# Layer norm sums moved, delta gates on GpSimd, beta behind the inverse, fills in eighths, two row turns held

## The reference, cut to what matters

```python
h = rms_norm(x, norm_w)
(aq, ak, av, az, c_glu, cz, dq, dk, dvv, dz, db, da, gate_logits) = split(h @ w_in)
# conformer branch
u = a * sigmoid(g);  u = causal_depthwise_conv(u, dw_w) + dw_b
u = layer_norm(u, ln_w, ln_b);  u = silu(u) * silu(cz);  y_c = u @ w_conv_out
# gated delta branch
q, k, v = silu(short_conv(dq | dk | dvv));  q, k = l2_normalize(q), l2_normalize(k)
beta = sigmoid(db)
g = -exp(a_log) * softplus(da + dt_bias)
# inside the delta rule, per head and chunk of rows; g is summed along the chunk
lower = strict((k * beta) @ k.T * decay);  tri = lower + eye
u, w = triangular_solve(tri, [v * beta, k * beta * exp(g)])
# merge
x = x + (g_a * y_a + g_c * y_c + g_d * y_d) @ w_out
```

## Time and profile before

| | us |
|---|---|
| median of 3 runs | 2552.84 |
| lowest, highest | 2544.14, 2553.32 |
| the profiled execution | 2549.82 |
| its span in the trace | 2548.0 |
| mean granted PE clock | 0.993 |

### The profile page before, as it was taken

The page is one execution under the profiler, slowest core; times in us unless marked ns, Lnnn a source line. Parts: engine busy times, 40 slices in busy tenths (PEclk is TensorE's granted clock), DMA queues, the critical chain, the costliest instruction groups (busy, mean ns, idle before and its releaser), DMA issues.

```text
span 2548.0 us, 42067 instructions
## 1 busy us (share of the span) xinstructions
PE 2484.7 (98%) x16588; PEld 2170.4 (85%) x16588; DVE 1171.3 (46%) x2176; ACT 1246.3 (49%) x2113; POOL 1455.7 (57%) x835
## 2 busy tenths in 40 slices
PE   7998999999999899999999999999999999999998
PEld 7997989888999788898777877778888878898998
DVE  8896645444878645536415613331101123535144
ACT  6467654355546764436544522443323345636543
POOL 6875746456977664544533343646565546464970
PEclk9999999999999899999999999999999999999999
DMA  6543343345544344335421022232222233235554
...
DMA packets 50601, 347.63 MB, mean 136 GB/s; under 512 B 5361, under 2 KB 8689, under 8 KB 8945
## 3 DMA queue, kind: packets, MB, share of 16 engines
...
HBM read 343.96 MB, written 1.05 MB: 135 GB/s over the span
## 4 chain that ended last, share of the span: by engine, by line
PE 91%; DVE 4%; ACT 3%; issue 1%; POOL 1%; DMA 1%; ACTq 0%; DVEq 0%; SPq 0%; POOLq 0%
PE pg L1948 23%; PE pg L1950 23%; PE pg L1949 23%; PE ps L2266 2%; PE pg L1971 2%; PE ps L2287 2%; PE ps L2285 1%; PE ps L2423 1%; PE ps L2404 1%; PE ps L2117 1%; ACT ring_hi L778 1%; PE ps L2123 1%; PE ps L2092 1%; PE ps L2504 1%; PE ps L2497 1%
## 5 line engine op out<-in xcount | busy, mean ns | idle before, releaser
L663 POOL TENSOR_TENSOR ring_lo<-ring,ring_hi 128x1024 fp32r<-128x1024 f32 (+3 forms) x502 | 1169.9, 2345 | 705.8 <-ACT ring_hi L778 704.8
L1948 PE MATMUL pg<-HH,ring_hi 128*128 128x256 f32 (+1 forms) x3264 | 1038.7, 318 | 8.1 <-POOL ring_lo L663 5.9
L1949 PE MATMUL pg<-HH,ring_lo 128*128 128x256 f32 (+1 forms) x3264 | 992.2, 304 | 0.0
L1950 PE MATMUL pg<-HL,ring_hi 128*128 128x256 f32 (+1 forms) x3008 | 920.0, 306 | 0.0
L1948 PEld LDWEIGHTS pg<-HH,ring_hi 128*128 128x128 f32 x3264 | 619.2, 190 | 73.8 <-issue 36.9
L1949 PEld LDWEIGHTS pg<-HH,ring_lo 128*128 128x128 f32 x3264 | 619.4, 190 | 43.4 <-issue 16.5
L1950 PEld LDWEIGHTS pg<-HL,ring_hi 128*128 128x128 f32 x3008 | 570.5, 190 | 28.3
L778 ACT ACTIVATE ring_hi<-ring 128x1024 fp32r<-128x1024 f32 (+3 forms) x572 | 563.8, 1003 | 30.3 <-DMA ring<-in_w_stream_dram 22.3
L788 ACT ACTIVATE take<-pg 128x256 f32<-128x256 f32 (+1 forms) x242 | 103.7, 429 | 452.6 <-PE pg L1950 445.0
L1950 PE MATMUL pg<-big_r,ring_hi 128*128 128x256 f32 (+1 forms) x928 | 299.3, 323 | 0.0
L1948 PE MATMUL pg<-big_r,ring_hi 128*128 128x256 f32 (+1 forms) x752 | 246.0, 327 | 3.9 <-DVE ring_lo L1633 2.7
...
## 6 DMA issues: line engine op xcount, KB each, us to landing
...
```

The source lines that it names most:

```text
L663: pool.tensor_tensor(ring_lo[:, slot, cols], ring[:, slot, cols], ring_hi[:, place * P:(place + n) * P].bitcast(F32), SUB).then_inc(sem(LO ...
L1948: first = pe.matmul(out, a[0], b[0], start=start, stop=False)
L1949: pe.matmul(out, a[1], b[0], start=False, stop=False)
L1950: return first, pe.matmul(out, a[0], b[1], start=False, stop=stop)
```

## The change

1. `LN_MEAN` goes from 20 to 18, so the ones-matmul of the mean stands ahead of chunk dn18, and the centering on DVE behind sconv(18). The square on ACT goes ahead of the drain of dn22, and DVE's sum of the squares ahead of sconv(22).
2. `delta_log` moves from DVE to POOL, behind the first cz chunk's `times_z`, as nine instructions; ACT gets one Exp more, which replaces the reciprocal. The sum along the rows becomes a chunk of its own, "decay", in the list at attention step 7, drained by ACT.
3. In the delta stretch the broadcast of beta goes. Beta multiplies the rows of the matrix of keys (four instructions on DVE) and the rows of v behind the inverse (ACT's copy, cut into heads, with a scale); VB is a plain copy.
4. dz, az and a_out are dealt in eighths, by weights (a part of a chunk 6, of a row 8, a turn 16), and `GAPS` changes.
5. `LATE_TURNS`: the turn of the "do" row of layer 0 stands behind norm 1's row, the turn of norm 5's row behind norm 6's.

```diff
+LATE_TURNS = {1: ("do", 0), 6: ("norm", 5)}
...
 def norm_mods(i, side):
 
     rows = [("mod", *x) for x in MOD_AT.get(("norm", i), [])]
-    return {"before": [("part", x) for x in rows[:1]] * 2, "after": rows, "turns": [("modt", *x[1:]) for x in rows]}[side]
+    late = [("modt", *x) for x in MOD_AT.get(LATE_TURNS.get(i), [])]
+    turns = [] if ("norm", i) in LATE_TURNS.values() else [("modt", *x[1:]) for x in rows]
+    return {"before": [("part", x) for x in rows[:1]] * 2, "after": rows + late, "turns": turns}[side]
...
 def att_fill(l):
-    return spread([("cz", l, m) for m in range(EARLY_CZ, KD)] + [("c_out", l, i) for i in range(2 * KD)], ATT_STEPS + LAG + 1)
...
-GAPS = [0.4, 1.0] + [1.9, 0.3] * 4 + [1.9, 0.7] + [1.6, 1.1, 1.0, 0.2]
+    fills = spread([("cz", l, m) for m in range(EARLY_CZ, KD)] + [("c_out", l, i) for i in range(2 * KD)], ATT_STEPS + LAG + 1)
+    fills[DECAY_STEP].append(("decay", l, 0))
+    return fills
...
+GAPS = [0.4, 1.0, 1.7, 0.3, 1.7, 0.9] + [1.7, 0.3] * 2 + [1.9, 0.7] + [1.6, 1.1, 1.0, 0.2]
...
-    return {"modt": 1}.get(name, 4)
+    return {"modt": 1, "dz": KD, "az": KD, "a_out": KD}.get(name, 4)
...
-    parts.insert(4, parts.pop(0))
+    parts.insert(KD, parts.pop(0))
+    work = [{"mod": 8, "modt": 16}.get((x[1] if x[0] == "part" else x)[0], 6) for x in parts]
...
-    at, end = 0, gaps[0]
-    for k, x in enumerate(parts):
-        while sum(gaps) * (k + 0.5) / len(parts) > end:
+    at, end, done = 0, gaps[0], 0
+    for x, w in zip(parts, work):
+        while sum(gaps) * (done + w / 2) / sum(work) > end:
             at += 1
             end += gaps[at]
+        done += w
         out[at].append(x)
...
-    return gates[:2] + [row] + gates[2:4] + [turn] + gates[4:]
+    return gates[:2] + [row] + gates[2:4] + ([turn] if l else []) + gates[4:]
...
-        LN_MEAN = 20
+        LN_MEAN = 18
+        LN_SQUARE = 22
...
+            def delta_log(l):
+                pool.wait_ge(sem("over_abs"), l + 1)
+                link(pool.tensor_scalar(NGC, B1, 1.0, None, ADD))
+                link(pool.tensor_scalar(NGC, NGC, -1.0, None, ADD))
+                link(pool.tensor_tensor(NGC, B1, NGC, SUB))
+                link(pool.tensor_tensor(NGC, NGC, GC, MUL))
+                link(pool.tensor_tensor(B2, B2, NGC, ADD))
+                link(pool.tensor_scalar(B0, B0, 0.0, None, MAX))
+                link(pool.tensor_tensor(B0, B0, B2, ADD))
+                link(pool.tensor_tensor(B0, B0, rep(EXA, NT), MUL))
+                pool.tensor_scalar(G, B0, -1.0, None, MUL).then_inc(sem("g_done"), 1)
...
                 for m in range(EARLY_CZ, KD):
                     times_z("cz", l, m, CV, CVH, CVL)
+                    if m == EARLY_CZ:
+                        delta_log(l)
...
                 act.wait_ge(sem("exp_abs"), l + 1)
                 act.activation(B2, B1, ACT.Ln, bias=1.0).then_inc(sem("ln_abs"), 1)
+                act.wait_ge(sem("ln_abs"), l + 1)
...
             def delta_decay(l):
-                act.wait_ge(sem("gc_ready"), l + 1)
-                act.activation(BEG, GCS, ACT.Exp).then_inc(sem("exp_gc"), 1)
+                sums = ready(CHUNK["decay", l, 0])[:, 0:2 * HEADS].rearrange("p (c h) -> p c h", c=NT)
+                act.activation(BEG, sums, ACT.Exp)
+                act.activation(NGC, sums, ACT.Copy, scale=-1.0).then_inc(sem("drained"), 1)
 
...
                 act.activation(NW, ps[:, 2, 0:2 * P].rearrange("p (a b) -> p a b", a=2), ACT.Copy, scale=-1.0)
-                act.activation(VN[:, 0:2 * P], ps[:, 2, 2 * P:4 * P], ACT.Copy).then_inc(sem("d_vn0"), 1)
+                for hh in range(2):
+                    ins = act.activation(VN[:, hh * P:(hh + 1) * P], ps[:, 2, (2 + hh) * P:(3 + hh) * P], ACT.Copy,
+                                         scale=BETA[:, 0, 2 * u + hh:2 * u + hh + 1])
+                ins.then_inc(sem("d_vn0"), 1)
...
+                    if j == LN_SQUARE:
+                        act.wait_ge(sem("ln_centered"), l + 1)
+                        act.activation(hn.rearrange("p (a b) -> p a b", a=KD), CV, ACT.Square).then_inc(sem("ln_sq"), 1)
...
-                act.wait_ge(sem("ln_centered"), l + 1)
-                act.activation(hn.rearrange("p (a b) -> p a b", a=KD), CV, ACT.Square).then_inc(sem("ln_sq"), 1)
...
-            def delta_log(l):
-                dve.wait_ge(sem("ln_abs"), l + 1)
-
-                link(dve.tensor_scalar(GC, B1, 1.0, None, ADD))
-                link(dve.tensor_scalar(NGC, GC, -1.0, None, ADD))
-                link(dve.tensor_tensor(NGC, B1, NGC, SUB))
-                link(dve.reciprocal(GC, GC))
-                link(dve.tensor_tensor(NGC, NGC, GC, MUL))
-                link(dve.tensor_tensor(B2, B2, NGC, ADD))
-                link(dve.scalar_tensor_tensor(B0, B0, 0.0, B2, MAX, ADD))
-                dve.wait_ge(sem("exp_a"), l + 1)
-                dve.scalar_tensor_tensor(G, B0, -1.0, rep(EXA, NT), MUL, MUL).then_inc(sem("g_done"), 1)
-
...
-                dve.wait_ge(sem("exp_gc"), l + 1)
-                dve.wait_ge(sem("beta"), l + 1)
-                link(dve.tensor_scalar(BETA, BETA, 0.5, 0.5, MUL, ADD))
-                link(dve.tensor_scalar(NGC, GCS, -1.0, None, MUL))
-                dve.tensor_tensor(BEG, BEG, BETA, MUL).then_inc(sem("gates_done"), 1)
+                dve.wait_ge(sem("drained"), DRAINED["decay", l, 0])
+                dve.tensor_scalar(BETA, BETA, 0.5, 0.5, MUL, ADD).then_inc(sem("gates_done"), 1)
                 dve.wait_ge(sem("gates_done"), l + 1)
...
-                    dve.tensor_scalar(UG[:, p * P:(p + 1) * P], C("until"), G[:, c, h:h + 1], None, MUL)
-                    ins = dve.tensor_scalar(IB[:, p * P:(p + 1) * P], ident, BETA[:, c, h:h + 1], None, MUL)
-                ins.then_inc(sem("d_ugib"), 1)
+                    ins = dve.tensor_scalar(UG[:, p * P:(p + 1) * P], C("until"), G[:, c, h:h + 1], None, MUL)
+                ins.then_inc(sem("d_until"), 1)
...
-            def pre_beta(l, u):
-                i = 4 * l + u
-                dve.wait_ge(sem("d_ib"), i + 1)
-                dve.wait_ge(sem("d_exp"), i + 1)
-                dve.tensor_tensor(LTS[u % 2], ps[:, 0 if u else 1, :], DTS[u % 2], MUL).then_inc(sem("d_lb"), 1)
-
             def pre_keys(l, u):
                 i = 4 * l + u
                 dve.wait_ge(sem("d_kk"), i + 1)
-                dve.wait_ge(sem("d_lb"), i + 1)
-                dve.tensor_tensor(LTS[u % 2], ps[:, 0 if u else 2, :], LTS[u % 2], MUL).then_inc(sem("d_lt"), 1)
+                dve.wait_ge(sem("d_exp"), i + 1)
+                for p in range(4):
+                    h, c = 2 * u + p // 2, p % 2
+                    s = slice(p * P, (p + 1) * P)
+                    ins = dve.scalar_tensor_tensor(LTS[u % 2][:, s], ps[:, 0 if u else 2, s], BETA[:, c, h:h + 1], DTS[u % 2][:, s], MUL, MUL)
+                ins.then_inc(sem("d_lt"), 1)
...
-                for p in range(4):
-                    h, c = 2 * u + p // 2, p % 2
-                    ins = dve.tensor_scalar(VB[:, p * P:(p + 1) * P], ps[:, 1, p * P:(p + 1) * P], BETA[:, c, h:h + 1], None, MUL)
-                ins.then_inc(sem("d_vb"), 1)
+                dve.tensor_copy(VB, ps[:, 1, :]).then_inc(sem("d_vb"), 1)
...
+                    if j == LN_SQUARE:
+                        dve.wait_ge(sem("ln_sq"), l + 1)
+                        dve.tensor_reduce(rstd[:, T:2 * T], hn.rearrange("p (m t) -> p t m", m=KD), AX.X, ADD).then_inc(sem("ln_sq_added"), 1)
                     sconv(l, j)
...
-                dve.wait_ge(sem("ln_sq"), l + 1)
-                dve.tensor_reduce(rstd[:, T:2 * T], hn.rearrange("p (m t) -> p t m", m=KD), AX.X, ADD).then_inc(sem("ln_sq_added"), 1)
...
-                    if it == 0:
-                        delta_log(l)
-                    if it == GATES_AT + 1:
+                    if it == DECAY_STEP + 1:
                         delta_decay(l)
...
+
+                j = CHUNK["decay", l, 0]
+                assert j == at["chunk"]
+                at["chunk"] += 1
+                bank_free(j)
                 pe.wait_ge(sem("g_done"), l + 1)
                 for c in range(NT):
-                    ins = pe.matmul(GCS[:, c, :], C("until"), G[:, c, :], start=True, stop=True)
-                ins.then_inc(sem("gc_ready"), 1)
+                    ins = pe.matmul(pg[:, j % 4, HEADS * c:HEADS * (c + 1)], C("until"), G[:, c, :], start=True, stop=True)
+                ins.then_inc(sem("chunk_ready"), 1)
...
                 if step == 0:
-                    pe.wait_ge(sem("d_ugib"), i + 1)
+                    pe.wait_ge(sem("d_until"), i + 1)
                     if u == 0:
                         pe.wait_ge(sem("hn_rms"), HN_BASE1(l) + ATT_N + 1)
                     pe.matmul(dst, ones, UG, start=True, stop=True).then_inc(sem("d_ug"), 1)
-                if step == 1:
+                if step == 2:
                     if u:
                         pe.wait_ge(sem("d_dt"), i + 1)
```

(33 more changed lines are left out.)

14 lines of the change are left out of this document (4 added, 10 removed).

## The result

| | us |
|---|---|
| changed kernel, median of 6 runs | 2560.57 (2560.14 to 2563.64) |
| before, median of 6 runs | 2552.29 (2544.14 to 2553.32) |
| ratio, 95% interval | 1.0043 (1.0028 to 1.0057) |
| profiled run of the changed kernel, its span | 2560.56, 2558.8 |
| profiled run before, its span | 2549.82, 2548.0 |

The change costs 8 us in the medians and 10.8 us between the two profiled spans. It lies within half a percent, as the forecast of 2554 did, but the extra time is three to four times the +2.8 that the sum gave.

A forecast was written before the change was run, and what follows sets the result against it. TensorE (PE) was taken as the bound, busy 2484.7 of 2548.0 us. The terms 4.6 - 2.0 - 7.7 + 3.6 + 4.6 - 0.3 gave +2.8: 2552.6 on the profiled run, 2555.6 on the median; forecast 2554, range 2539 to 2567.

The forecast's parts named there:

- Layer norm: Ahead of dn18 PE waits 5.6 us for VectorE's sum, the old 3.3 us wait goes; two layers, +4.6 us.
- Gates: Two PE waits, 3.9 us a layer, go, but GpSimd's chain lets PE gain only 1.0; -2.0 us (-4.6 to +7).
- with the low clock behind that as now: Gates step: PE idles within c_out1 for GpSimd, and the low clock behind costs as before; no extra size given.
- Delta: Delta stretch: broadcast matmuls gone -6.9, fewer odd mod parts -2.0, v's copy in halves +1.2; -7.7 us (-9 to -5).
- slower rival: Delta stretch: eighths uncover the chain, 24 gaps stall 0.5 us each, +12 us to 2566; chance 0.16.
- Norm 1: The held turn brings a third weights split, waiting for its load, ahead of the table load; +3.6 us.
- Norm 6: Third split ahead of the table load 3.5, low clock 2.0, a GpSimd wait of 0.9 gone; +4.6 us.
- "do" and norm 5: Where the turns stood: nothing gained in layer 0's "do", a GpSimd wait being there anyway; -0.3 us at norm 5.

The follow-up runs named there:

- e1: Changed kernel with LN_MEAN back at 20, the early square kept; 2546.6 us, ratio 0.9992 to the kernel before.
- e9: Changed kernel, mean still at dn18, both turns in their old places, nine small GpSimd instructions behind the last cz chunk; 2546.5 us, ratio 0.9992 to before.
- e3: Changed kernel with GpSimd's nine small instructions behind the last cz chunk's products, not the first's; 2554.9 us, ratio 1.0024 to the kernel before.
- e7: Kernel before with only beta moved behind the inverse, fills still in quarters with old GAPS; 2548.3 us, ratio 0.9995 to the kernel before.
- e2: Changed kernel with both row turns back in their old places; 2553.6 us, ratio 1.0021 to the kernel before.
- e4: Changed kernel with turns held, but two weight splits instead of three ahead of the table load at norms 1 and 6; 2554.6 us, ratio 1.0028 to before.
- e5: Changed kernel with LN_MEAN at 20, both turns in old places, nine GpSimd instructions behind the last cz chunk; 2530.2 us, ratio 0.9926 to the kernel before.
- e6: Kernel before with only points 3 and 4 of the change; 2544.8 us, ratio 0.9984 to the kernel before.
- e8: Kernel before with points 3 and 4 and the early square, gates left on VectorE; 2533.4 us, ratio 0.9934 to the kernel before.

## Why the prediction was right, and where its sum failed

The range (2539 to 2567) and the sign of the sum hold, and each wait stands where the text put it. The range owes its success in part to its width of 28 us: the sum gave 2.8 of the 10.8 us. By term, from the two profiles:

- **Layer norm: +4.6 forecast, +7.7 measured** (+4.3 and +3.4). What the term speaks of came as forecast: up to dn19 the new wait and the low clock behind it cost 7.4 and 7.5 us, the old wait and its low clock gave 5.1 and 6.2 back, net +2.3 and +1.3 beside 2.3 for each. From where dn18 would have started to L2369 it is 5.3 us and not 5.6, as the reduction took 3.63 us and not 3.94 (the 4.74 of the row counts from the end of the matmul ahead). What failed is that I followed only the layer norm's own instructions. ScalarE's queue, with a split that waits for its load, brought a second wait (0.94 for the row's drain) with its own low clock: +2.0 and +2.1. e1 and e9 show that all of it hangs on this step, 8.1 to 8.7 us a layer between dn18 and dn20.
- **Gates: -2.0 forecast, +3.5 measured** (+1.7 and +1.8). GpSimd's nine instructions take 2.74 us; the line through two larger forms gave 2.8. The wait in c_out1 was said to be 3 to 5 us and is 3.9, and PE reaches the matmul behind it 1.8 us sooner than before, where I had 1.0. The step that failed is "with the low clock behind that as now", by which I let the old and the new low clock cancel. They can't: the old one lay ahead of the point at which GpSimd's chain sets the time, so that to lose it only lengthens the new wait; the new one lies behind that point and is paid in full. From the matmul at 274.38 on PE lost 3.5 us more in each layer. By the term's own numbers it should have been -1.0 + 2.0 a layer. e3 measures the pair: 1.9 us less of wait, 4.7 us less of time.
- **Delta: -7.7 forecast, -7.7 measured** (-3.8 and -3.9), but not for the reasons given. e7 shows that without the eighths 4.6 us of the 6.9 are lost again, 1.8 in one layer to stalls that the list shows; the eighths were priced at 2.0 for odd mod parts and are worth 5.4. Two errors that cancel, so this number is luck. The slower rival, eighths that uncover the chain, is refuted: they cover it.
- **Norm 1: +3.6 forecast, +3.5 measured. Norm 6: +4.6 forecast, +4.0 measured.** The third split, its wait on the DMA (3.09 and 3.19 us) and the table load behind it are as worked out; shifts ahead of it taken off, the table load starts 4.2 us later than before at both, where I had 3.6 and 3.5. About 0.9 of norm 6's time goes with a low clock that e2, e4, e5, e6 and e9 show there without a third split. In the profile before the clock was 1.00, and that was the exception: e7 and e8 had half clock there too (0.83 over ten us, 0.72 over six), but their stage was no longer than before.
- **"do" and norm 5: 0 and -0.3 forecast, 0 and -0.3 measured** for the turns. The -1.5 in "do" is clock behind a wait for GpSimd that both kernels have (1.1 us before, 2.0 after; the clock over 562 to 567 was 0.69 before), and e5, e7 and e9, which leave the turn there, have it too. In e2, e6 and e8, which also leave it, the clock fell as before; in the four kernels that hold the turn it never did, so a part of the change in this is not excluded.
- The start's +1.5 is no part of the change: the same wait of 2.2 us at 41 us, with low clock behind it in seven of the kernels' profiles (0.72 in the changed kernel) and with full clock in four (1.00 before and in e5, e7 and e9).

The sum of the rows is +10.7, the difference of the spans (10.8) but for rounding. So of the missing 8 us, 5.5 are the gates and 3.1 the layer norm, less 0.6 at norm 6; the start and "do" cancel.

What stays open: why the same wait brings the clock down in one execution and not in the next; why the one load in e3 and e8 was slow; and why ScalarE is late for the row with the mean at dn18 and not with it at dn20. None of these was tried.
